# One inference step of a hybrid SSD / S5 / hierarchical-MoE decoder: 520 columns instead of 536 behind the recurrences, and a new order of TensorE's short products

## The reference

```python
xp = jnp.concatenate([meta, x_prompt], axis=1)            # 16 + 512
xn = _rmsnorm(x, norm_mix);  proj = xn @ w_in             # z, xbc, dt, u
xbc, new_conv = _causal_conv(xbc, conv_prefix, conv_w, conv_b)
y, new_ssm = _ssd_chunked(xs, dt, -jnp.exp(a_log), bm, cm, d_ssd, ssm_h0, chunk)
y_ssd = _rmsnorm(y * jax.nn.silu(z), ssd_norm)
# S5: state h scanned along the tokens for 64 groups, then
y = jax.nn.gelu(y);  y = y * jax.nn.sigmoid(y @ w_glu + b_glu);  y_s5 = _rmsnorm(y, gain)
x = x + jnp.concatenate([y_ssd, y_s5], axis=-1) @ w_out
x = x + _hier_moe(_rmsnorm(x, norm_ffn), ...)             # 4 groups x 8 experts, top 2 of one group
y_prompt = _rmsnorm(xp, norm_final)[:, N_META:];  y_sample = _rmsnorm(xs, norm_final)
```

## Time and profile before

| | us |
|---|---|
| median of 3 runs | 1067.53 (1066.47 to 1075.4) |
| the profiled execution | 1061.96 |
| its span (first to last instruction) | 1059.7 |
| TensorE busy | 961.3 (91%) |
| VectorE, ScalarE, GpSimd busy | 434.8, 331.1, 268.0 |
| HBM read, written | 260.17 MB, 25.61 MB |

### The profile page before, as it was taken

One profiled execution on the slowest core, in us unless ns is written; L12 is line 12 of the kernel. 1 busy time (PEld: TensorE's weight loads), 2 busy tenths in 40 slices (PEclk: granted clock), 3 DMA queues, 4 the chain that ended last, 5 costly groups with the idle time before them and its releaser, 6 DMA issues.

```text
span 1059.7 us, 17219 instructions
## 1 busy us (share of the span) xinstructions
PE 961.3 (91%) x6496; PEld 682.0 (64%) x6497; DVE 434.8 (41%) x743; ACT 331.1 (31%) x662; POOL 268.0 (25%) x510
## 2 busy tenths in 40 slices
PE   6999999999999999999999999999877788998881
PEld 5889779877776788998765555555443444554440
DVE  6999877454466898951521111111100101111112
ACT  3025323453325784322422222232212121222113
POOL 1000888888421010000012222222222112222110
PEclk9999999999999999999999999999999999999996
DMA  7585172110098744255589999999999999999994
GB/s 268 125 142 92 29 121 81 41 63 22 12 223 226 254 147 175 87 238 239 218 323 392 396 383 398 385 394 397 395 396 395 396 413 404 409 410 408 425 385 167
DMA packets 73566, 277.54 MB, mean 262 GB/s; under 512 B 36953, under 2 KB 38873, under 8 KB 56497
## 3 DMA queue, kind: packets, MB, share of 16 engines
q1 hardware_dynamic: 63020, 252.67, 65.0%
q0 software_dynamic: 8720, 19.86, 6.8%
q10 hardware_dynamic: 1780, 4.41, 1.1%
HBM read 260.17 MB, written 25.61 MB: 270 GB/s over the span
## 4 chain that ended last, share of the span: by engine, by line
PE 68%; DMA 23%; DVE 5%; issue 2%; ACT 1%; POOL 0%; SPq 0%; ACTq 0%; POOLq 0%; DVEq 0%
PE ps L653 24%; DMA sb_arena<-w_up 20%; PE ps L1023 9%; PE ps L1037 7%; PE ps L1016 7%; PE ps L919 7%; PE ps L992 2%; DMA sb_arena<-ssm_in 2%; PE ps L685 1%; PE ps L741 1%; PE ps L798 1%; DVE sb_arena L1960 1%; PE ps L772 1%; PE ps L895 1%; PE ps L1030 1%
## 5 line engine op out<-in xcount | busy, mean ns | idle before, releaser
L653 PE MATMUL ps<-sb_arena 128*128 128x264 f32 (+1 forms) x1152 | 266.9, 392 | 9.1 <-DMA sb_arena<-wi 9.1
L653 PEld LDWEIGHTS ps<-sb_arena 128*128 128x128 f32 x1152 | 218.8, 191 | 57.5 <-DMA sb_arena<-wi 9.6
L1956 DVE TENSOR_TENSOR sb_s5b<-sb_s5b,ps 128x256 f32<-128x256 f32 x36 | 22.2, 617 | 408.0 <-PE ps L1023 408.0
L1023 PE MATMUL ps<-sb_arena 128*64 128x256 f32 x1152 | 131.3, 380 | 22.0 <-DMA sb_arena<-w_up 22.0
L1037 PE MATMUL ps<-sb_arena 128*64 128x512 f32 x576 | 131.5, 598 | 20.7 <-DVE sb_arena L1960 20.7
L1016 PE MATMUL ps<-sb_arena 128*64 128x256 f32 x1152 | 132.6, 383 | 16.5 <-DMA sb_arena<-w_gate 15.8
L1016 PEld LDWEIGHTS ps<-sb_arena 128*64 128x64 f32 x1152 | 83.6, 138 | 76.3 <-DMA sb_arena<-w_gate 27.0
L1023 PEld LDWEIGHTS ps<-sb_arena 128*64 128x64 f32 x1152 | 82.5, 137 | 67.1 <-DMA sb_arena<-w_up 28.9
L1388 ACT ACTIVATE sb_kxf<-ps,sb_gate_of 64x512 f32<-64x512 f32 x36 | 24.6, 683 | 301.1 <-PE ps L1037 301.1
L1037 PEld LDWEIGHTS ps<-sb_arena 128*64 128x64 f32 x576 | 39.0, 136 | 90.1 <-issue 60.9
L1415 DVE TENSOR_TENSOR sb_arena<-sb_arena 128x64 f32<-128x64 f32 (+12 forms) x86 | 78.0, 907 | 19.5 <-DMA sb_arena<-ssm_in 12.2
(11 more groups left out here) (308 smaller groups left out, 1210.3 us busy)
## 6 DMA issues: line engine op xcount, KB each, us to landing
sb_arena<-w_gate SPq DMA_DIRECT2D x32, 2048.0 KB, 33.7
sb_arena<-w_up SPq DMA_DIRECT2D x32, 2048.0 KB, 35.9
sb_arena<-w_down SPq DMA_DIRECT2D x32, 2048.0 KB, 35.6
sb_arena<-wi SPq DMA_DIRECT2D x28, 512.0 KB, 4.0
sb_arena<-w_out SPq DMA_DIRECT2D x4, 2048.0 KB, 8.5
sb_arena<-ssm_in POOLq DMA_DIRECT2D x8, 512.0 KB, 8.9
sb_arena<-wglu SPq DMA_DIRECT2D x8, 512.0 KB, 5.0
o_ssm_s<-sb_arena POOLq DMA_DIRECT2D x8, 512.0 KB, 4.0
```

The source lines that it names most:

```text
L653: last = mm(ps[:, b0 + h, 0:t1 - t0], ring[w % 3][:, k, :], src[:, k, t0:t1], start=k == 0, stop=k == KD - 1)
L1023: last = mm(ps[64 * r:64 * r + 64, 1, 0:256], xt[:, k, :], Wu[s][:, k, 256 * r:256 * r + 256], start=k == 0, stop=k == KD - 1)
L1956: V.tensor_tensor(hh.rearrange("p (j c) -> p c j", j=2), sg.rearrange("p (c j) -> p c j", j=2), ps[:, 1, 0:256].rearrange("p (c j) -> p c ...
```

## The change

* **Columns.** z, the gate, Gelu, the gated product, the sums of squares, the projection, the router and the experts go over columns 16 to 535 (two halves of 260, `HALVES_T`) instead of all 536. Tables, scratches and token tiles (`TR`) have 520 rows. Two VectorE operations mask out what stands behind row 520. By the reference's routing of these inputs that takes 32 (token, expert) rows of 1072 away, and two experts with 66 and 68 rows get along with one tile: 34 tiles instead of 36.
* **Short products spread.** The last 8 toeplitz rounds go one by one between the k-steps of wide block 17, the decay sums into block 18, the samples' dt into block 19, and the y of SSD chunk 4 into block 30. On ScalarE and VectorE the exponentials of the decays (`dE`) move behind one more conv block.
* **S5 outputs.** Wide block 25 moves from ahead of the two `state_outputs` stretches to behind them. GpSimd reports the state before it works on the samples. SP issues the ring loads 26 and 27 ahead of the y store, and 28 behind it.
* **End.** SP waits for the last real tile's scatter itself (`yst`) instead of for a report of GpSimd at the end of its loop (`ye_ready`). ScalarE's expert loop has two more waits on its own earlier instructions.

```diff
+NT = N - META
+HALF = NT // 2
+HALVES_T = ((META, META + HALF), (META + HALF, N))
+TR = [(i * P, min(P, NT - i * P)) for i in range(5)]
+REST = TR[4][1]
...
-MAXT = E + (2 * N) // (T + 1)
+MAXT = E + (2 * NT) // (T + 1)
...
+            ring_load(26)
+            ring_load(27)
             y_store(0)
-            for w in range(26, 29):
-                ring_load(w)
+            ring_load(28)
...
-            sp.wait_ge(ye_ready, 1)
-            for i, (t0, n) in enumerate(TT):
+            rows_done = tile_bound(sp, slice(E, E + 1), E)
+            sp.wait_ge(yst, rows_done * 16)
...
+            pl.sem_inc(h_done, 1)
             h0v = HA[:, COL_S0:COL_S0 + NS]
...
             nc.gpsimd.tensor_tensor(sst[:], sst[:], smp, ALU.add).then_inc(h_done, 1)
-            pl.wait_ge(h_done, 1)
+            pl.wait_ge(h_done, 2)
...
-            pl.sem_inc(ye_ready, 1)
...
+                    if w == 17:
+                        toeplitz_round(8 + k)
+                    if w == 18 and k < 5:
+                        decay_sums(k)
+                    if w == 19:
+                        sample_steps(2 * k)
                     if w == 28:
                         pe.wait_ge(gelu_done, k + 1)
-                    for h, (t0, t1) in enumerate(HALVES):
+                    if w == 30:
+                        ssd_y(4, k)
+                    for h, (t0, t1) in enumerate(HALVES if w < 20 else HALVES_T):
...
-            pe.wait_ge(t_ld, 16 * 32)
-            for rd in range(16):
+            def toeplitz_round(rd):
+
...
-            for c, (t0, n) in enumerate(CH):
+            def decay_sums(c):
+
...
-            last.then_inc(cs_mm, 1)
+                if c == 4:
+                    last.then_inc(cs_mm, 1)
...
+            def sample_steps(first):
+
+                for h in range(first, first + 2):
+                    r, i = h % 2, h // 2
+                    last = mm(ps[64 * r:64 * r + 64, 6, 256 + i * NS:256 + (i + 1) * NS],
+                              dtv[0:24, 4, h:h + 1].broadcast_to([24, HD]), cst[0:24, C_ID + 16:C_ID + 24],
+                              start=True, stop=True)
+                if first == HEADS - 2:
+                    last.then_inc(ds_mm, 1)
+
+            pe.wait_ge(t_ld, 16 * 32)
+            for rd in range(8):
+                toeplitz_round(rd)
             for w in range(17, 20):
...
 
-            def ssd_c(c):
...
+                    if c:
+                        mm(y_half, Yo[0:n, h, :], ident[0:n, 0:n], start=True, stop=False)
+                    last = mm(y_half, xdt[0:n, h, :], Lm[0:n, h, 0:n], start=c == 0, stop=True)
+                if i == 7:
+                    last.then_inc(y_mm, 1)
+
+            def ssd_states(c):
+
+                n = CH[c][1]
                 pe.wait_ge(sa_eva, c + 1)
                 for g in range(2):
                     last = mm(ps[:, 6 + g, :], btok[0:n, g, :], xde[0:n, 8 * g:8 * g + 8, :], start=True, stop=True)
                 last.then_inc(st_mm, 1)
+
+            def ssd_c(c):
+
+                for i in range(8):
+                    ssd_y(c, i)
+                ssd_states(c)
 
...
             ssd_y_off(2)
-            wide(25)
             pe.wait_ge(yo_ev, 4)
             state_outputs(0, 8)
             ssd_c(2)
             state_outputs(8, 8)
+            wide(25)
             ssd_a(3)
...
             wide(29)
-            ssd_c(4)
-            for w in range(30, 36):
+            wide(30)
+            ssd_states(4)
+            for w in range(31, 36):
                 wide(w)
...
                         for h in range(2):
-                            last = mm(ps[:, 2 * (o % 2) + h, 0:HALF], w_[:, k, c:c + P], y_[:, k, HALF * h:HALF * h + HALF],
+                            last = mm(ps[:, 2 * (o % 2) + h, 0:HALF], w_[:, k, c:c + P], y_[:, k, HALVES_T[h][0]:HALVES_T[h][1]],
...
             decays(0)
+            raw_evac(8 + 10)
+            conv_silu(8)
             ac.wait_ge(de_in, 2)
             act_(dE, dE, ACT.Exp).then_inc(de_out, 1)
-            for i in range(10, XBC):
-                raw_evac(8 + i)
-                conv_silu(i - 2)
+            raw_evac(8 + 11)
+            conv_silu(9)
...
-                act_(zT[:, w - 20, 0:SPLIT], ps[:, b0, 0:SPLIT], ACT.Copy)
-                act_(zT[:, w - 20, SPLIT:N], ps[:, b0 + 1, 0:N - SPLIT], ACT.Copy).then_inc(wide_free[w % 2], 1)
+                for h, (t0, t1) in enumerate(HALVES_T):
+                    last = act_(zT[:, w - 20, t0:t1], ps[:, b0 + h, 0:HALF], ACT.Copy)
+                last.then_inc(wide_free[w % 2], 1)
...
-                act_(yg[:, i, 0:NP_].rearrange("p (m j) -> p j m", j=J),
-                     yraw[:, i, 0:NP_].rearrange("p (j m) -> p j m", j=J), ACT.Gelu_apprx_tanh)
+                act_(yg[:, i, META:NP_].rearrange("p (m j) -> p m j", j=J),
+                     yraw[:, i, 0:NP_].rearrange("p (j m) -> p m j", j=J)[:, META // J:], ACT.Gelu_apprx_tanh)
...
+                    ac.wait_ge(silu, q + 1)
...
+                    ac.wait_ge(staged, q + 1)
...
+            conv(9)
             dv.wait_ge(cs_mm, 1)
...
-            for i in range(9, XBC):
+            for i in range(10, XBC):
                 conv(i)
...
-            tt(iomv, bc(iom, 1, 5), bc(cst[:, C_VAL:C_VAL + 5], 2, E), ALU.mult)
+            stt(valt, cst[:, C_TOK:C_TOK + 5], float(NT), cst[:, C_VAL:C_VAL + 5], ALU.is_lt, ALU.mult)
+            tt(iomv, bc(iom, 1, 5), bc(valt, 2, E), ALU.mult)
...
             link(V.reciprocal(gate[:, 0, :], rm))
+            tt(gate[:, 0, :], gate[:, 0, :], valt, ALU.mult)
             tt(gate[:, 1, :], gate[:, 0, :], rdif, ALU.mult)
```

More of the change, by code:

```diff
@@ L172, in build @@
         sig = part(30832, KD, N)
-        sq4, sqsum = part(8208, 4, N), [part(44016 + N * i, N) for i in range(2)]
+        sq4, sqsum = part(8208, 4, NT), [part(44016 + NT * i, NT) for i in range(2)]
         root_b = sqsum
@@ L208, in build @@
         Ob = small(5 * E // 2).bitcast(BF16).rearrange("p (i e) -> p i e", e=E)
-        rm, m1, m2, r5, rdif = (small(5) for _ in range(5))
+        rm, m1, m2, r5, rdif, valt = (small(5) for _ in range(6))
         assert rt[0] <= 9920
@@ L222, in build @@
         x1 = [part(1024 * i, D) for i in range(4)] + [kxf[:, 0:D]]
-        x1T = [part(19040 + N * d, N) for d in range(6)] + [kxf[:, D + N * u:D + N * u + N] for u in range(2)]
-        sqx = kxf[:, D + 2 * N:D + 3 * N]
+        x1T = [part(19040 + NT * d, NT) for d in range(6)] + [kxf[:, D + NT * u:D + NT * u + NT] for u in range(2)]
+        sqx = kxf[:, D + 2 * NT:D + 3 * NT]
         iomv = kxf[:, 2 * D + 608:2 * D + 608 + 5 * E].rearrange("p (i e) -> p i e", e=E)
@@ L492, in _ @@
             sp.wait_ge(xs_st, 80)
-            for i, (t0, n) in enumerate(TT):
+            for i, (t0, n) in enumerate(TR):
                 sp.dma_start(sum_scr[t0:t0 + n, :], x1[i][0:n]).then_inc(sum_st, 16)
@@ L807, in ssd_y_off, with ssd_y @@
                        start=True, stop=True).then_inc(yo_mm, 1)
-            def ssd_c(c):
+            def ssd_y(c, i):
                 n = CH[c][1]
-                pe.wait_ge(sa_evd, c + 1)
-                if c:
-                    pe.wait_ge(yo_ev, 2 * c)
-                for i in range(8):
-                    if i % 4 == 0:
-                        pe.wait_ge(m_done, 2 * c + 1 + i // 4)
-                    for r in range(2):
-                        h = 2 * i + r
-                        y_half = ps[64 * r:64 * r + 64, 4 + i // 4, (i % 4) * P:(i % 4) * P + n]
-                        if c:
-                            mm(y_half, Yo[0:n, h, :], ident[0:n, 0:n], start=True, stop=False)
-                        last = mm(y_half, xdt[0:n, h, :], Lm[0:n, h, 0:n], start=c == 0, stop=True)
-                last.then_inc(y_mm, 1)
+                if i == 0:
+                    pe.wait_ge(sa_evd, c + 1)
+                    if c:
+                        pe.wait_ge(yo_ev, 2 * c)
+                if i % 4 == 0:
+                    pe.wait_ge(m_done, 2 * c + 1 + i // 4)
+                for r in range(2):
+                    h = 2 * i + r
+                    y_half = ps[64 * r:64 * r + 64, 4 + i // 4, (i % 4) * P:(i % 4) * P + n]
+                    if c:
+                        mm(y_half, Yo[0:n, h, :], ident[0:n, 0:n], start=True, stop=False)
[3 more added lines that the diff above has]
+            def ssd_states(c):
+                n = CH[c][1]
                 pe.wait_ge(sa_eva, c + 1)
```

81 lines of the change are left out of this document (38 added, 43 removed).

## The result

The changed kernel takes 1086.5 us (1085.5 to 1087.5, 4 runs), the one before 1067.0 us (1065.4 to 1075.4, 4 runs): 1.0167 times as long, 95% interval 1.0112 to 1.0221. It is slower, and beyond the range of 1058 to 1075. A second series of it (experiment 5) gave 1086.5 again, 1.0173 (1.0099 to 1.0248).

The account below looks back on a forecast made before the run. DMA was taken to bound the experts' stretch, TensorE what precedes it. TensorE's shift of +1.9 at the projection's end, −2.1 for experts and −0.4 at the end gave −0.6 us: 1067.0 on the median's scale, range 1058 to 1075.

Parts of the forecast that it names:

- The end: End of the program: SP waits for the scatter itself instead of GpSimd's report, −0.4 us (−0.1 to −0.6).
- Chunk 4 behind block 30: Late chunk 4 y delays VectorE, GpSimd's store and ScalarE; TensorE waits 2.4 us ahead of block 34 (0 to 5).
- Rival B: Clock falls behind the new waits, 1.7 us of work each, from about 2.5 us of wait; 1076; chance 0.12.
- Short products spread: Short products between wide blocks' k-steps: +0.3 us for block 30 (0 to 0.6), nothing for blocks 17 and 18.
- Chunk 0: Third decay product 2.5 us later: samples' dt 1.0, a table load 1.28, small weight loads in block 19 0.3.
- The S5 waits: S5 outputs behind chunk 2's off-diagonal products: TensorE waits for VectorE, +0.9 and +2.05 us (second 1.5 to 3).
- Gelu: Blocks 28 and 29: less wait for Gelu, −0.5 us (0 to −0.7).
- Columns: Fewer columns: wide blocks 20 to 35 give 3.5 us, 0.22 each; projection −1.3 (bounds 0 and −2.85).
- Experts: Expert stretch: 32 rows fewer to gather and scatter, −2.1 us (bounds −1.0 and −3.2).

Follow-up runs that it names:

- experiment 5: The changed kernel run again without an edit, on the second chip: 1086.5 us (1084.2 to 1089.4).
- experiment 1: Changed kernel with GpSimd's tile loop meant to stop behind the last real tile (one of two empty tiles went): 1079.0 us, −7.5.
- experiment 2: Changed kernel with SP's ring loads 31 and 32 ahead of its wait for the last SSD state and that state's store: 1080.7 us, −5.8.
- experiment 4: Changed kernel with wide block 25 back ahead of the S5 outputs and SP's y store ahead of ring loads 26 to 28: 1079.2 us, −7.3.
- experiment 9: Changed kernel with wide block 25 behind the first two rounds of the S5 outputs and their wait for VectorE: 1081.9 us, −4.6.
- experiment 6: Changed kernel with the 16 products of the samples' dt in one row behind wide block 19: 1082.7 us, −3.8.
- experiment 7: Changed kernel with the samples' dt products in two groups of eight, ahead of block 19's k-steps 0 and 4: 1086.5 us.
- experiment 8: Changed kernel with ScalarE's exponential of dE ahead of block 18's emptying: 1084.1 us, −2.4.

## Why the prediction was wrong, point by point

The forecast was −0.6 us, measured were +19.5 (+25.8 between the two profiled spans, of which 1.1 came ahead of the change). Two steps failed altogether: the end, where the sum had no term for GpSimd's empty tiles, and chunk 4, where it left out SP's queue. One cause was given the small chance (the clock), and one term was mis-sized (the short products).

* **The end.** The sum had −0.4 for SP's wait, and that came: −0.7. It took no account of GpSimd's loop in fours, though the description of the kernel before has it: 34 tiles make two empty ones, which this engine gathers and scatters one behind the other while the norm runs, and the program doesn't end without it. The two tiles that go were taken as a gain only; the end that they bring cost 7.5 us (experiment 1). Before, 36 tiles were a full number of fours.
* **Chunk 4 behind block 30.** The step followed VectorE's lateness down GpSimd's and ScalarE's queues, and found a stall of 2.4 us ahead of block 34. That stall exists (2.58 in experiment 2). The step left out the third queue: SP's own wait for the same state, with the weights of block 31 behind it. Before, that load went out at 362.63, 4.6 us ahead of block 31, and came just in time. Now it went out 21.4 us later, TensorE stood 6.45 us until 4.7 us behind it, and the granted clock was then 0.50 until 394. Undone: −9.8 us in the trace, −10.4 by the medians, 2.3 of it the interleaving.
* **Rival B** had the mechanism of the clock and the places right (it names these waits), and its threshold and its size wrong. It was put at 1.7 us for a fall, and "from about 2.5 us of wait on". The clock fell behind 1.77 us. And 1.7 us is the price in front of wide products: in front of 75-column products it stayed down 13.6 us and cost 5.7 (experiments 4 and 9). The prediction's own sign of being wrong, a granted clock of 0.50 behind one of these waits, was the right one to look for.
* **Short products spread.** The term was +0.3 for block 30, and 0.3 inside that of block 19. It is 0.27 to 0.29 us for each of the eight changes where the short products' weights fill a part of the array (24 x 64 and 16 x 64): 2.2 in block 19 (experiments 6, 7), 2.3 in block 30. For the toeplitz rounds and decay sums (128 x 128) nothing, as forecast.
* **Chunk 0.** Table load and lost cover came as worked out: the wait at the third product grew by 1.55 (1.45 of it the load, experiment 8), and a wait of 0.89 stands ahead of the first. With the 2.2 above and a fall of the clock in the profiled run (1.7) they are 6.3 of the 6.5 that chunk 0 added.
* **The S5 waits** came as forecast, 0.79 and 1.77 against 0.9 and 2.05.
* **Gelu.** −0.5 was expected. The blocks 28 and 29 took 15.9 us instead of 15.25, with 0.85 of wait ahead. ScalarE no longer waits for y in between (0.58 us at 343.44 before), but block 28 takes one tile of Gelu for each k-step, and a tile of 512 + 8 columns now took 1.12 us (352.83 to 353.95) where one of 528 + 8 had taken 1.01 (339.67 to 340.68), 0.9 us more for eight. The change also has Gelu read and write in another order of its dimensions; that this is the cause was not tested. Gelu can't start earlier, either: in both kernels it follows chunk 4's exponentials and its table load on ScalarE at once.
* **Columns.** Wide blocks as forecast (7.06 us each). From the projection's first product to the first one of another kind behind its last block, 106.3 us (427.69 to 533.97) instead of 109.2 (404.67 to 513.83), −2.9: all of the projection's share came through, and the −1.3 was too careful. The rule of the Trainium skill ("TensorE: Matmul & The Clock Gate", on LDWEIGHTS) that the prediction weighed and set aside would have been nearer.
* **Experts:** −1.1 instead of −2.1 in this profile, at the bound for tiles, and not clear of noise. From the first expert product to SP's load of the sums, with the 0.7 of SP's wait in it, the thirteen profiles with 34 tiles took 502.2 to 505.3 us, the one before 504.5 (1043.35 − 538.82). No gain in the experts is shown.

## What to carry to other kernels

When an instruction is moved behind a wait, list every engine that waits for its result, the one that only issues DMAs too, and then what stands behind that wait in its queue. When a count changes, look at every loop that rounds it up: empty turns are free on an engine that is done early, and at the end of the program they cost what reaches beyond the other engines' work. A short wait costs its length and can cost the slow clock of what follows as well, so if there must be one, put wide products behind it and not a long row of narrow ones.
